# A two-layer encoder trunk: index keys, index weights and forget logits in one block of 104 columns, two forgetting query blocks ahead of the index logits

## The reference

```python
z = x @ w_in            # iq 256, ik 64, iw 4, fq 512, fk 512, fv 512, ff 8 columns, and others
iq = apply_rope(iq.reshape(B, S, IDX_HEADS, HEAD_DIM), cos, sin)     # 4 index heads of 64
ik = apply_rope(ik, cos, sin)                                        # one index key for all heads
logits = einsum('bqhd,bkd->bqhk', iqb, ik)
score = einsum('bqh,bqhk->bqk', iwb, relu(logits))                   # then top_k(score, 128)
log_f = log_sigmoid(ff + b_forget); c = cumsum(log_f)                # forgetting attention
```

## Time and profile before

| | us |
|---|---|
| median of three runs | 2491.82 |
| lowest, highest | 2487.12, 2491.95 |
| the profiled execution: its own time | 2488.1 |
| its span, first to last instruction | 2486.3 |
| TensorE busy | 2107.3 (85%) |
| VectorE busy | 911.2 (37%) |
| ScalarE busy | 549.5 (22%) |
| granted TensorE clock, mean over the span | 0.934 of full |

### The profile page before, as it was taken

How to read it: one execution, slowest core, us unless ns; L and a number is a source line. 1 busy time by engine, 2 the same in 40 slices (tenths; PEclk the granted TensorE clock), 3 DMA queues, 4 the chain that set the end, 5 groups by cost and what they waited for, 6 DMA issues and landing times.

```text
span 2486.3 us, 29712 instructions
## 1 busy us (share of the span) xinstructions
PE 2107.3 (85%) x9820; PEld 1191.1 (48%) x9820; DVE 911.2 (37%) x1764; ACT 549.5 (22%) x1168; POOL 227.7 (9%) x369
## 2 busy tenths in 40 slices
PE   4999998999958888788579999999998698778882
PEld 3776775776433223222257767757744232222231
DVE  5765644544331111011268564544434211110114
ACT  2344244143010100000033422533421000000000
POOL 0000001000011111111100000100001111111112
PEclk9999998999979989899879999999999798998996
DMA  5211410413269999999632114114143699999993
GB/s 184 91 69 35 136 68 35 136 69 119 93 238 408 400 413 409 407 417 414 251 124 102 35 68 136 35 69 135 46 175 137 265 400 410 410 407 407 419 410 129
DMA packets 96860, 541.44 MB, mean 218 GB/s; under 512 B 19011, under 2 KB 21827, under 8 KB 72161
## 3 DMA queue, kind: packets, MB, share of 16 engines
q1 hardware_dynamic: 76576, 504.75, 51.3%
q0 software_dynamic: 12864, 25.20, 2.9%
q10 hardware_dynamic: 7296, 9.97, 1.6%
HBM read 524.66 MB, written 23.07 MB: 220 GB/s over the span
## 4 chain that ended last, share of the span: by engine, by line
PE 57%; DMA 20%; DVE 11%; issue 6%; ACT 3%; ACTq 1%; POOL 1%; DVEq 0%; SPq 0%; POOLq 0%
PE ps L895 11%; DMA xslot<-in_w_up 9%; PE ps L637 7%; PE ps L639 7%; PE ps L638 7%; PE ps L911 7%; PE ps L823 5%; PE ps L837 4%; DMA ring<-in_w_up 3%; DMA wslot<-in_w_up 3%; DMA scr<-in_w_up 3%; PE ps L739 2%; PE ps L790 2%; DMA scr<-scr 2%; PE ps L761 2%
## 5 line engine op out<-in xcount | busy, mean ns | idle before, releaser
L1736 DVE TENSOR_TENSOR scr<-scr,ps 64x512 f32<-64x512 f32 x64 | 44.2, 691 | 876.5 <-ACT scr L1215 876.5
L637 PE MATMUL ps<-hT_lo,w_hi 128*128 128x512 f32 (+1 forms) x832 | 339.1, 408 | 22.3 <-DVE w_lo L1273 14.3
L639 PE MATMUL ps<-hT_hi,w_hi 128*128 128x512 f32 (+1 forms) x832 | 327.0, 393 | 0.0
L638 PE MATMUL ps<-hT_hi,w_lo 128*128 128x512 f32 (+1 forms) x832 | 326.2, 392 | 0.0
L895 PE MATMUL ps<-ring,scr 128*64 128x512 f32 x512 | 240.8, 626 | 39.8 <-issue 21.2
L1019 ACT ACTIVATE scr<-ps 128x512 f32<-128x512 f32 (+3 forms) x334 | 151.9, 456 | 503.5 <-PE ps L911 400.0
L896 PE MATMUL ps<-ring,scr 128*64 128x512 f32 x512 | 238.5, 621 | 0.0
L1039 ACT ACTIVATE w_hi<-ring 128x1024 fp32r<-128x1024 f32 x124 | 130.6, 1053 | 392.1 <-PE ps L639 319.6
L1273 DVE TENSOR_TENSOR w_lo<-ring,w_hi 128x1024 fp32r<-128x1024 f32 x124 | 150.8, 1216 | 106.7 <-ACT w_hi L1039 99.5
L637 PEld LDWEIGHTS ps<-hT_lo,w_hi 128*128 128x128 f32 (+1 forms) x832 | 156.8, 188 | 63.7 <-issue 13.9
L823 PE MATMUL ps<-scr,ring 128*128 128x512 f32 x384 | 170.6, 606 | 3.3 <-ACT scr L1019 3.3
(11 more groups left out here) (223 smaller groups left out, 2848.8 us busy)
## 6 DMA issues: line engine op xcount, KB each, us to landing
ring<-in_w_down SPq DMA_DIRECT2D x32, 2048.0 KB, 28.5
ring<-in_w_gate SPq DMA_DIRECT2D x32, 2048.0 KB, 33.6
ring<-in_w_up SPq DMA_DIRECT2D x32, 2048.0 KB, 33.3
ring<-in_w_in SPq DMA_DIRECT2D x30, 2048.0 KB, 8.1
xslot<-in_w_gate SPq DMA_DIRECT2D x16, 2048.0 KB, 32.3
xslot<-in_w_up SPq DMA_DIRECT2D x16, 2048.0 KB, 31.7
xslot<-in_w_down SPq DMA_DIRECT2D x16, 2048.0 KB, 27.6
scr<-in_w_gate SPq DMA_DIRECT2D x8, 2048.0 KB, 30.6
```

Of the source, the lines that this page charges most:

```text
L637: mm(out, a[0], b[1], start=first, stop=False)
L638: mm(out, a[1], b[0], start=False, stop=False)
L639: return mm(out, a[0], b[0], start=False, stop=last)
```

## The change

The index key's 64 columns are no longer there twice. The unit `ik` now has 104 columns: keys (0 to 63), index weights (from 64), forget logits (from 96). The unit `iwff` is gone, so a layer has 24 matmuls less. ScalarE copies the 64 rows of keys twice out of PSUM, to partitions 0 to 63 and 64 to 127 of `z`, under a new semaphore `ik_copied`; VectorE waits for it before it reads index weights and forget logits from the same bank, and does so ahead of the rotation of `ik`. Two units, `fq0` and `fq1`, are projected ahead of the index logits, in PSUM banks 4 and 5, where it was one. The load of `fv` now waits for the `w_lo` of the unit `ik`, which is the last index unit.

```diff
--- before.py
+++ after.py
@@ -358,19 +359,19 @@
-        IDX_W, IWT, FFT = 424, 32, 64
+        IDX_W, IWT, FFT = 360, 64, 96
 ...
-        units = [(name, q) for name in pieces if name[1:] != "br" and name[:2] != "wo" for q in range(4)]
+        units = [(name, q) for name in pieces if name[1:] != "br" and name[:2] != "wo" for q in range(3 if name == "idx" else 4)]
 ...
-                return idx_cols[:, :, q * P:(q + 1) * P] if q < 3 else idx_cols[:, :, 352:IDX_W]
+                return idx_cols[:, :, q * P:min((q + 1) * P, IDX_W)]
@@ -474,8 +475,8 @@
                     for src, dst in ((w_in[one, :, COL["iq"]:COL["iw"]], idx_cols[:, :, 0:320]),
-                                     (w_in[one, :, COL["ik"]:COL["iw"] + 32], idx_cols[:, :, 320:416]),
-                                     (w_in[one, :, COL["ff"]:COL["ff"] + 8], idx_cols[:, :, 416:424])):
+                                     (w_in[one, :, COL["iw"]:COL["iw"] + 32], idx_cols[:, :, 320:352]),
+                                     (w_in[one, :, COL["ff"]:COL["ff"] + 8], idx_cols[:, :, 352:360])):
@@ -506,7 +507,7 @@
-                            sp.wait_ge(lo_ready.sem, lo_ready.at((name, 3), l))
+                            sp.wait_ge(lo_ready.sem, lo_ready.at((name, 2 if name == "idx" else 3), l))
@@ -669,15 +670,16 @@
                 def index_logits(l):
-                    projected(["iq0", "iq1", "ik"], l, "idx")
-                    w = unit("idx", 3, l)
+                    projected(["iq0", "iq1"], l, "idx")
+                    w = unit("idx", 2, l)
 ...
-                        ins = split_product(bank[b].t[0:IDX_W - 352, :], w(k), hT(k), k == 0, k == KD - 1)
-                    filled(ins, b, "iwff")
-                    project(("fq", 0), l, "fq", 0, 4)
+                        ins = split_product(bank[b].t[0:IDX_W - 2 * P, :], w(k), hT(k), k == 0, k == KD - 1)
+                    filled(ins, b, "ik")
+                    for n in range(2):
+                        project(("fq", n), l, "fq", n, 4 + n)
                     pe.wait_ge(roped.sem, roped.at("ik", l))
@@ -700,7 +702,7 @@
-                        projected([(name, n) for n in range(KB)], l, name, int(name == "fq"))
+                        projected([(name, n) for n in range(KB)], l, name, 2 * int(name == "fq"))
@@ -1056,8 +1058,15 @@
-                    copy(z[r % 2], b, bank[b].t, scale)
-                    in_sbuf(b, key, l)
+                    if key == "ik":
+
+                        for half in range(2):
+                            nc.scalar.activation(z[r % 2][half * HD:(half + 1) * HD, :], bank[b].t[0:HD, :],
+                                                 ACT.Copy).then_inc(ik_copied.sem, ik_copied.tick("ik"))
+                        act.wait_ge(ik_copied.sem, ik_copied.at("ik", l))
+                    else:
+                        copy(z[r % 2], b, bank[b].t, scale)
+                        in_sbuf(b, key, l)
@@ -1178,10 +1187,13 @@
                     for n, key in enumerate(("iq0", "iq1", "ik")):
-                        split_to(("idx", min(n + 2, 3)), l)
+                        if n < 2:
+                            split_to(units[n + 2], l)
                         take_z(key, l)
                     split_to(("fq", 1), l)
                     plain(("fq", 0), qT[:, 0, :], l, SCALE)
+                    split_to(("fq", 2), l)
+                    plain(("fq", 1), qT[:, 1, :], l, SCALE)
@@ -1676,15 +1688,15 @@
                         split_to(units[r + 2], l)
+                        if key == "ik":
+                            b_iw = book.where.get("ik", 0)
+                            dve.wait_ge(ik_copied.sem, ik_copied.at("ik", l))
+                            V.tensor_scalar(iwT, bank[b_iw].t[IWT:IWT + IDX_H, :], (IDX_H * HD) ** -0.5, None,
+                                            ALU.mult).then_inc(iwT_ready.sem, iwT_ready.tick("iwT"))
+                            dve.wait_ge(small_land.sem, small_land.at("all", l))
+                            V.tensor_scalar(ffx, bank[b_iw].t[FFT:FFT + 8, :], b_f[FFT:FFT + 8, 0:1], None,
+                                            ALU.add).then_inc(bank[b_iw].read, 1)
                         rope(r, key, key, dst, l)
-                    split_to(("fq", 1), l)
-                    b_iw = book.where.get("iwff", 0)
-                    filled(b_iw, "iwff", l)
 ...
```

More of the change, by code:

```diff
@@ L384, in unit_end @@
             if name == "idx":
-                return ("iq0", "iq1", "ik", "iwff")[q]
+                return ("iq0", "iq1", "ik")[q]
             if name[1:] == "v" and q < 3:
```

10 lines of the change are left out of this document (3 added, 7 removed).

## The result

The changed kernel takes 2499.33 us, the median of five runs (2494.43 to 2503.08). The kernel before, run beside it, takes 2490.09 (2480.79 to 2491.95). These two medians are 9.2 us apart. The ratio on record with them is 1.0057 with a 95% interval from 1.0042 to 1.0073: some 14 us slower (10 to 18). Forecast was 2494, 4.0 us over the kernel before. The sign was right, and the median lies within the stated range (2487 to 2501). The size was wrong, and the favoured case, "no change", wasn't what came. The profiled execution took 2494.43 us, the lowest of the five, so the profile shows less than the medians: its span is 2492.6, 6.3 over the span before.

A forecast was written before the change was run, and what follows sets the result against it. VectorE was taken as the bound from the first logits to `fk2`. Per layer `fq2` 0.19 us later plus 2.03 of clock gave 2.22, counted as 2.0; twice, +4.0 us. Forecast 2494 us, range 2487 to 2501.

The forecast's parts named there:

- the favoured case, "no change": Whole kernel: no change told apart by the measurement, 0.63, against slower 0.30 and faster 0.07.
- The block that goes gives nothing, since the `w_lo` of `fq2` stands behind the scores: Behind the index logits: TensorE idles some 4.9 us; of the 5.57 us only 0.61 are left.
- `fq2` starts 11.93 us after the logits: Index part: logits' start to `w_lo` of `fq2` takes 11.80 us, TensorE starts 0.13 later; 12.54 before.
- The second copy delays `fq1` by 0.58 us: ScalarE's route to the logits: 0.60 us for the second key copy, so TensorE starts `fq1` at 66.4, not 65.82.
- The turn of `iq0` lands 7.6 us behind its first issue, TensorE waits 1.3 us, and that "costs nothing more" by the clock: Ahead of `fq0`: the `fv` load meets the turning DMAs, bounds 4.67 and 9.36 after the load's issue; logits 0.8 us later.
- The rule on this collision: Turn of `iq0` against the load: by the rule almost undisturbed, sum some 0.4 us less; the prediction went by the row.
- The clock behind the long idle stretch costs 2.03 us at TensorE: Behind the 4.9 us idle stretch: lower clock in the next 7 us loses 2.03 us, bounds 0 and 2.73.
- Register instructions at nothing: Attentions: some 75 more on TensorE, at most 0.08 us each, taken as nothing; as rival +5 to +10 us, chance 0.04.
- Everything behind follows the index part: Behind `fk1`: forget sums, `fk2` and all behind follow by 2.0 us a layer, +4.0 us in all.
- Rival "the turn waits for the whole load": Ahead of `fq0`: VectorE goes on at 60.66, logits 6.0 us later, +15 us, 2503; decides above 9.5 us; chance 0.07.
- Where the runs fall: Whole kernel: runs fall in two places about 4.5 us apart, 2487.1 and 2491.9; the new median may be at either.
- One of the signs of being wrong that I had named: Index part: wrong if logits start over 2 us later, `fq2` starts with the logits' end, or the clock holds.

The follow-up runs named there:

- e3: Changed kernel with 20 further matmuls, whose results nobody reads, in TensorE's idle stretch behind the index logits; ratio 1.0045.
- e11: Changed kernel, but the `fv` load waits for the rotation of `ik` and VectorE does `w_lo` of `fq2` ahead of the index scores; ratio 1.0011.
- e1: Changed kernel, but the load of `fv` waits for the rotation of `ik`; ratio 1.0037.
- e12: The changed kernel as it is, measured and profiled again against the kernel before; ratio 1.0057, median 2499.98 us.
- e2: Changed kernel, but VectorE does the `w_lo` of `fq2` ahead of the index scores; ratio 1.0053.
- e10: Changed kernel with `fq1` in PSUM bank 7 instead of 5 and another start of the banks' turn, 121 register instructions less on TensorE; ratio 1.0033.
- e5: Kernel of e1 with `fq1` in PSUM bank 7 instead of 5 and the banks' turn started at 2 instead of 0; ratio 1.0026.
- e7: Changed kernel with only `fq0` ahead of the logits, the late `fv` load, and `w_lo` of `fq1` behind the rotation of `ik`; ratio 0.9973.
- e4: Kernel before with `fq0` in PSUM bank 5 instead of 4, 52 register instructions more on TensorE; ratio 1.0009.
- e9: Kernel before with the banks' turn behind the index logits started at 1 instead of 0, 50 register instructions less on TensorE; ratio 1.0000.

## Why the prediction was wrong, point by point

- *The block that goes gives nothing, since the `w_lo` of `fq2` stands behind the scores:* right. Idle 5.06 us in both layers where I had 4.9; e3 and e11 fill or remove it.
- *`fq2` starts 11.93 us after the logits:* 12.20. VectorE needs 10.85 us from the logits' start to this `w_lo`, not 10.57. 0.27 us a layer under.
- *The second copy delays `fq1` by 0.58 us:* right, 0.65 in e1.
- *The turn of `iq0` lands 7.6 us behind its first issue, TensorE waits 1.3 us, and that "costs nothing more" by the clock:* this step failed. VectorE went on after 8.96 and 8.24 us, TensorE waited 2.42 and 1.71 us, and in one layer of two the clock fell behind it, for 1.5 us. The second profile, of e12, has 8.38 and 9.07 us, waits of 1.85 and 2.53, and again a fall behind the longer one. The logits start 3.49 and 1.34 us later, not 0.8: 3.2 us of the difference for both layers together. I had a disturbed turn of 7.37 us in the earlier trace rows and a bound of 9.36 beside it, and put the value next to the former. The trace of the kernel before held dearer ones, which I passed over: 7.75 us at the same place in the second layer, and, with a load that went out 1.52 us ahead of the turn at 276.18, 7.91 and 8.14 in the two layers (the first one's reader is the row below). And I took the 1.97 us of the earlier trace rows without a loss of clock for proof that a wait there costs only itself, though by my own 1.3 us of wait a landing 0.7 us later led past it. The two errors add up: each microsecond of landing is one of wait, and behind the longer waits the clock takes 1.5 more.

```profile
284.09 0.69 DVE L1349 TENSOR_TENSOR scr<-scr 128x512 f32<-128x512 f32 x1 [4.86 <-DMA scr<-scr]
```

- *The rule on this collision:* the Trainium skill, "DMA: Bandwidth & Descriptors", section "Queues, rings and completion order", has each DMA engine take a packet from each queue in turn, and so I read it that the small DMAs would pass almost undisturbed. The traces speak against "almost undisturbed", here more than at the earlier trace rows: 8.24 to 9.83 us in the ten profiled layers with the load 0.7 us behind the turn (changed kernel, e2, e3, e10, e12), against 4.67 and 5.12 before, where no load met it. They don't contradict the rule itself, which names no time: see the last rival.
- *The clock behind the long idle stretch costs 2.03 us at TensorE:* it costs 2.8 and 2.1, and by e3 1.8 and 1.2 at `fk2`. I had counted 2.0 there. About right, for the reason given.
- *Register instructions at nothing:* right in the attentions of branch f and the sparse branch, to 0.1 us in 86.5 and 83.4. That the choice of banks does nothing elsewhere is not shown: see e5 and e10.
- *Everything behind follows the index part:* this is where the rest went. A turn in branch d stands near to where the clock falls (behind it TensorE was idle for 1.27 and 1.54 us before, without a fall; the shortest with one is 2.05), and in the changed kernel the first layer fell over it. I had the earlier trace rows from that very stretch as a price for the index part, and never asked what that place does itself when all of it moves.
- *Rival "the turn waits for the whole load":* it named the place and, at 9.5 us, a point that e10 passes (9.83 and 9.82 us; idle 3.31 and 3.29 us; the clock fell in both). As a mechanism it is wrong: in the eight of the ten layers whose traces have the load's landing (e2, e3, e10, e12), the turned block lands 1.5 to 3.3 us before the load does. The turn is slowed and overtakes. Its price of +15 us is near the 14 measured by luck: it had the logits 6.0 us later in each layer, and they were 3.5 and 1.3 later. And I had drawn it as a case apart, where the ten layers spread evenly from 8.24 to 9.83 us.
- *Where the runs fall:* I had read three runs as two places, 2487.1 and 2491.9. With more runs they aren't there: the 24 of the kernel before beside e12 spread from 2479.3 to 2493.6 us.

One of the signs of being wrong that I had named came: the logits started more than 2 us later in one layer. And the turn of `iq0` landed past the 7 to 8 us that I had named.

Terms together, both layers: forecast 4.0; the logits' start adds 3.2; 0.5 by VectorE's scores; the rest up to `fk2` adds 1.1 (2.70 and 2.06 us between `fq2` and `fk2`, where I had 1.8); up to the experts 1.6. That is 10.4 of the 14, and it agrees with the profiled sum of 10.5 (12.1 in e12). The largest single error is the landing of the turn and the clock behind it. What the ratio shows beyond these terms stays open.

## What to carry to other kernels

Removing work from an engine pays only where that engine is the bound, and which one it is changes with the order: the same 24 matmuls were worth nothing or worse with two blocks ahead of the logits, and 2.7 us a layer at the first attention (4.4 at `fk2`) once the load went out late and one `w_lo` stood behind the rotation (e7). When a wait is moved earlier on a load's queue, list the small transfers that it will now meet and take the dearest collision in the trace, in all layers, as the price, and still leave room above it: here it would have been 8.14 us, and 8.24 to 9.83 came. Then add to each idle stretch that comes near the length after which the clock fell elsewhere in the trace its price in clock, as a second term. And when you measure an edit at a mark, put the mark behind the next idle stretch: a fall of the clock just behind it doesn't show.

## What the runs showed of the hardware

- Four DMAs of 64 KB each, issued over 2.4 to 4.1 us, let their reader go on 3.9 to 5.2 us after the first issue when alone, and in the attentions' projections 6.4 to 9.0 us when a 2 MB load of another queue was issued 0.9 to 1.9 us behind them, and 7.7 to 9.3 us when it was issued 1.5 us ahead of them. With the load 0.69 us behind, ahead of `fq0`, it was 8.2 to 9.8 us, and in the eight of these ten layers whose traces have the load's landing still 1.5 to 3.3 us before it. Why the landing varies by 1.6 us at one place stays open.
- Ahead of `fq0`, in the ten layers with an early load, TensorE's clock held behind 1.71 and 1.85 us of idle time and fell behind 1.92, 2.10, 2.42 and the longer ones. Elsewhere length alone doesn't tell: behind the 1.9 us ahead of `fk2` it held in both profiles of the changed kernel and fell in both layers of e11, behind 2.25 us in branch d of e7 it held in one layer and behind 2.21 it fell in the other, and behind 2.75 us it held ahead of `fk2` in e3 and fell ahead of `fq3` in e2 and e11.
- With 20 useless matmuls in the idle stretch the clock stayed at 1.00. `fk2` came 1.2 to 1.8 us earlier by them.
- The bank into which a block is projected changes no data and no order, and still moved the time by 2 us (e4) or 6 us (e10 against e12), or not at all (e9), with the attentions of branch f and the sparse branch as long as ever. A part that does show is the stretch from the logits to `fq2`: 12.2 us in the changed kernel, 11.6 in e5 and e10.
